# Attention stage: a third place for groups of key pages, and one ring of four PSUM banks for what PE turns or scores

## The chip, the core and the metric

The kernel runs on one core of a Trainium2 chip. The metric is the device time of one execution in microseconds (us). Five engines work side by side, each in its own written order: PE (TensorE, matrix products and transposes), DVE (VectorE), ACT (ScalarE), POOL (GpSimd) and SP (SyncE, which here only issues DMAs). They meet through semaphores. PE writes only to PSUM, which has eight banks of 512 fp32 columns on 128 partitions; DVE and ACT copy results out of it.

## What is computed

One step of a decoder layer with two branches, sparse attention and a recurrent one (RWKV), for a prompt of 1024 rows and for 8 batches of 8 new rows each, which also look back on 2048 cached keys. The change touches only the attention of both. Its part of the reference, cut to what matters:

```python
def _sparse_attention(q, k_sel, v_sel, dist, rel_bias):
    ...
    logits = jnp.einsum('bthd,btkhd->bthk', q, k_sel).astype(jnp.float32) * ATT_SCALE
    logits = logits + jnp.moveaxis(bias, -1, -2)
    logits = jnp.where(valid[:, :, None, :], logits, -jnp.inf)
    probs = jax.nn.softmax(logits, axis=-1)
    return jnp.einsum('bthk,btkhd->bthd', probs.astype(v_sel.dtype), v_sel)
```

The kernel does not gather the selected keys: an earlier stage makes a mask, and the attention runs over all keys with the mask added. For the new rows, keys and values lie in pages of 128 rows of a cache in HBM, and a page table says which 16 pages belong to a batch.

## The kernel before, in words

The program is a row of stages with barriers between them. The attention stage (`attention`, L1735 on) lies between the recurrent branch and the merge with the MLP. It weaves two bodies of work on every engine.

**The prompt.** For each of four pairs of heads `i`: q, k and v come by DMA, PE turns v and k into rows (L1945, three groups each, kept by ACT at L2101 as `v_rows`, `k_rows`). Then come 8 tiles `t` of 128 queries: logits (PE L1906), mask and bias and row maximum (DVE L2192 to L2208), exp (ACT L2108), the turn of the probabilities (PE L1914, one group of up to four 128x128 transposes per head and 512 keys), their copy to `probs_T` (ACT L2101), and the product with v (PE L1926) and with the inverse row sum (PE L1932).

**The sample.** For each of 8 batches `b` there are four groups `j` of four key pages, numbered `J = 4b + j`. SP loads a group into `k_pages` (four DMAs of 256 KB, L1835), which has two places, so that group `J` may be loaded when PE has turned group `J-2` (`k_turned`). PE turns a group in four steps `c` (`turn_keys`, L1977), into the two banks `k_group_T_ps`; DVE copies the even steps (L2253), ACT the odd ones (L2142). `scores` (L1990) multiplies by the queries into the one bank `group_logits_ps`, and DVE masks it (L2267, L2268). `scores_new` (L1996) does the 64 new keys in the same bank. After the exp of the batch (ACT L2152), five groups of probabilities are turned in the same bank again (L2008, L2011), copied by DVE (L2301, L2303) and ACT (L2159), and multiplied by the value pages (L2026). The 16 value pages of a batch are loaded at L1848, a quarter when the same quarter of the batch in front has been used (`v_used`). The mask of a batch is loaded at L1858 when the last batch's masks are done (`masked_new`).

**Banks.** `turn_ps` has one bank for all turns of the prompt: a turn waits until ACT has copied the turn in front (`free_turn`). `k_group_T_ps` has two, `group_logits_ps` one, `logits_ps` two, `att_ps` and `sample_att_ps` one each: eight in all.

**The order.** Every engine's body is a set of generators, each yielding a place on one axis before each piece, and `weave` merges them by that number. One unit is one batch of the sample; a pair of heads takes 2.11 units. On PE key step `c` of group `j` stands at `b + 0.2 j + 0.05 c`, its scores at b plus 0.30, 0.52, 0.72 or 0.92, `scores_new` at `b + 0.93`, the probabilities from `b + 1.10`, the values from `b + 1.34`. On SP the key group stands at `b + 0.2 j - 0.18`, the values at `b + 0.37` (0.65 for the first batch), the mask at `b - 0.03`, the pair's v at `2.11 i - 0.35` and its k and q at `2.11 i - 0.01`. SP issues strictly in that order, so that a wait there holds back all behind it.

## Time and profile before

| | us |
|---|---|
| median of 3 runs | 2878.05 |
| lowest and highest | 2874.58, 2878.06 |
| the profiled execution | 2863.94 |
| its span on the core | 2862.2 |
| attention, from PE's first turn to its last | 1357.5 to 1790 |

The page gives each engine's busy time over the span; the stages differ, so the views that matter are those cut to the attention stage: busy time by stretch, what each engine waited for, and the instructions in order of time. In these, a row of PE is a group of equal matrix instructions with its start, its length, and in brackets how long PE was idle before it and what released it. The granted clock is given as a share of TensorE's full 2.4 GHz; it has two levels, 0.50 (1.2 GHz) and 1.00. The profiled execution lies 14 us under the median of the timed runs.

### The profile page before, as it was taken

What the parts mean: (1) busy time and instruction counts of PE and PEld (TensorE: products, weight loads), DVE (VectorE), ACT (ScalarE), POOL (GpSimd) and SP (SyncE); (2) the same over time, 40 slices, a digit from 0 to 9 for tenths busy, and PEclk for the clock granted to TensorE, in tenths of its full rate; (3) what the DMA queues carried; (4) which work ended last, traced back from release to release, by engine and by line L of the source; (5) the groups of instructions that cost most, each with busy time, mean ns of one, the idle gap of its engine ahead of it and who ended that gap; (6) DMA issues with size and microseconds to landing.
All of it is one profiled execution on the core that took longest, in us unless ns stands there. A gap on an engine that the chain in (4) does not pass through costs nothing. (4 is left out here: it accounts for less than half of the span.)

```text
span 2862.2 us, 52506 instructions
## 1 busy us (share of the span) xinstructions
PE 2516.2 (88%) x21869; PEld 1821.2 (64%) x21869; DVE 1467.6 (51%) x2995; ACT 554.9 (19%) x1170; POOL 92.7 (3%) x133
## 2 busy tenths in 40 slices
PE   6989999777877878876867877999999999999998
PEld 4566666445555456554544545778888888888886
DVE  3449999851642722714634544575543443443543
ACT  3211000022212312321433433212200100100101
POOL 0110000000100100100100100000000000000000
PEclk9989999888898987988988999999999999999999
DMA  5414222231321311212754663631111111111111
GB/s 166 116 27 154 76 76 76 82 116 33 91 75 57 84 58 55 80 32 76 249 190 144 215 208 108 215 107 45 45 30 45 44 45 40 34 45 45 45 30 70
DMA packets 289078, 252.39 MB, mean 88 GB/s; under 512 B 53527, under 2 KB 240505, under 8 KB 288718
## 3 DMA queue, kind: packets, MB, share of 16 engines
q1 hardware_dynamic: 208502, 187.67, 21.8%
q10 hardware_dynamic: 80344, 61.41, 7.2%
q8 instruction: 173, 2.83, 0.4%
q14 instruction: 59, 0.48, 0.1%
HBM read 200.43 MB, written 48.59 MB: 87 GB/s over the span
## 5 line engine op out<-in xcount | busy, mean ns | idle before, releaser
L502 PE MATMUL first_banks<-hT,w_pr 128*128 128x384 f32 (+3 forms) x1392 | 442.1, 479 | 5.3 <-PEq L178 5.3
L502 PEld LDWEIGHTS first_banks<-hT,w_pr 128*128 128x128 f32 (+1 forms) x1392 | 265.0, 192 | 176.7 <-issue 24.5
L989 PE MATMUL rwkv_banks<-h_chunk,w_gate 128*128 128x384 f32 (+1 forms) x768 | 298.3, 534 | 29.1 <-ACT gate_rows L1326 13.3
L2436 DVE TENSOR_TENSOR x<-x,ps_mm 128x272 f32<-128x272 f32 x280 | 120.9, 436 | 308.1 <-PE ps_mm L2403 308.0
L989 PEld LDWEIGHTS rwkv_banks<-h_chunk,w_gate 128*128 128x128 f32 x768 | 155.8, 214 | 124.6 <-issue 57.2
L2403 PE MATMUL ps_mm<-merged_then_hidden,w_mm 128*128 128x272 f32 x960 | 227.1, 393 | 1.6 <-DVE sums_of_right_sides L2656 0.9
L2403 PEld LDWEIGHTS ps_mm<-merged_then_hidden,w_mm 128*128 128x128 f32 x960 | 182.2, 190 | 39.9 <-DVE sums_of_right_sides L2656 1.3
L2403 PE MATMUL ps_mm<-v_T_and_gates_then_h_mlp,w_mm 128*128 128x272 f32 x864 | 204.5, 392 | 0.0
L2427 ACT COPY merged_then_hidden<-ps_mm 128x272 f32<-128x272 f32 x160 | 61.7, 386 | 721.2 <-PE ps_mm L2403 721.2
L2403 PEld LDWEIGHTS ps_mm<-v_T_and_gates_then_h_mlp,w_mm 128*128 128x128 f32 x864 | 164.1, 190 | 33.9
L751 DVE TENSOR_SCALAR_CACHE_REDUCE idx_pages<-scores,mid 128x384 f32<-128x384 f32 (+1 forms) x180 | 170.2, 946 | 6.4
L2403 PE MATMUL ps_mm<-sums_of_right_sides,w_sums_mm 128*128 128x272 f32 x704 | 165.3, 392 | 0.2 <-DVE sums_of_right_sides L2614 0.2
L2403 PEld LDWEIGHTS ps_mm<-sums_of_right_sides,w_sums_mm 128*128 128x128 f32 x704 | 133.7, 190 | 28.1 <-issue 0.6
L2436 DVE TENSOR_TENSOR merged_then_hidden<-merged_then_hidden,ps_mm 128x272 f32<-128x272 f32 x120 | 51.5, 434 | 195.2 <-PE ps_mm L2403 195.2
L1977 PE MATMUL k_group_T_ps<-ident,k_pages 128*128 128x128 f32 x512 | 91.7, 309 | 44.4 <-DMA k_pages<-in_cache_k 44.4
L2403 PE MATMUL ps_mm<-att_T,w_sums_mm 128*128 128x272 f32 x544 | 128.1, 392 | 0.0
L2403 PEld LDWEIGHTS ps_mm<-att_T,w_sums_mm 128*128 128x128 f32 x544 | 103.4, 190 | 21.3
L1977 PEld LDWEIGHTS k_group_T_ps<-ident,k_pages 128*128 128x128 f32 x512 | 65.0, 157 | 72.3 <-DMA k_pages<-in_cache_k 47.5
L2253 DVE COPY k_group_T<-k_group_T_ps 128x512 f32<-128x512 f32 x64 | 44.1, 689 | 106.4 <-PE k_group_T_ps L1977 106.0
L617 ACT COPY stage_pr<-first_banks 128x384 f32<-128x384 f32 (+1 forms) x72 | 33.4, 464 | 325.6 <-PE first_banks L502 325.6
L2403 PE MATMUL ps_mm<-sums_of_right_sides,w_mm 128*128 128x272 f32 x352 | 84.8, 393 | 1.6 <-DVE merged_then_hidden L2436 1.6
L2403 PEld LDWEIGHTS ps_mm<-sums_of_right_sides,w_mm 128*128 128x128 f32 x352 | 66.7, 190 | 16.1 <-DVE merged_then_hidden L2436 2.5
(443 smaller groups left out, 3684.3 us busy)
## 6 DMA issues: line engine op xcount, KB each, us to landing
k_pages<-in_cache_k SPq DMA_DIRECT2D x128, 256.0 KB, 3.1
v_pages<-in_cache_v SPq DMA_DIRECT2D x128, 256.0 KB, 4.6
w_gate<-in_w_in ACTq DMA_DIRECT2D x48, 512.0 KB, 4.0
w_mm<-in_w_mlp_in SPq DMA_DIRECT2D x32, 512.0 KB, 5.4
w_mm<-in_w_mlp_out SPq DMA_DIRECT2D x32, 512.0 KB, 5.3
w_pr<-in_w_in SPq DMA_DIRECT2D x27, 512.0 KB, 6.0
proj_T<-stage_pr ACTq DMA_DIRECT2D x24, 548.0 KB, 5.6
v_T_and_gates_then_h_mlp<-gates_T SPq DMA_DIRECT2D x16, 544.0 KB, 4.7
```

What stands on the lines that cost most here:

```text
L502: ins = MM(B[0:width, 6 + q % 2, 0:m], wk[:, k, 0:width], p.hT[:, k, t0:t0 + m], start=(k == 0), stop=(k == KO - 1))
L617: nc.scalar.copy(dst[:, t0:t0 + m], B[0:width, 6 + q % 2, 0:m]).then_inc(S["kept"], 1)
L751: ch.mark(nc.vector.tensor_scalar(above[0:m, 0:x.shape[1]], x, mid[0:m, j:j + 1], 0.0, ALU.is_gt, ALU.add, accum_out=cnt[0:m, j:j + 1]))
L989: ins = MM(B[:, GB, 0:w], gw[:, n % 2, k, :], hc[:, k, 0:w], start=(k == 0), stop=(k == KO - 1))
L1977: ins = nc.tensor.transpose(KT[:, c % 2, g * 128:g * 128 + 128], kp[:, J % 2, g, c * 128:c * 128 + 128], p.ident[:, :])
L2253: V.tensor_copy(ktb[:, J % 2, c, :], KT[:, 0, :]).then_inc(S["kt_dve"], 1)
L2403: ins = self.nc.tensor.matmul(self.ps[:, c, self.BANK[step], 0:272], left[step][:, k, :], right[step][:, k, 272 * c:272 * c + 272], start= ...
L2427: self.nc.scalar.copy(self.target(step, rows, c), self.out(act, u, step, c)).then_inc(self.by_act, 1)
L2436: self.nc.vector.tensor_tensor(to, to, ps, ALU.add).then_inc(self.by_dve, 1)
```

## The change

`k_pages` gets three places. SP puts every key group 0.2 units earlier (`-0.38` for `-0.18`), and waits for the turn of group `J-3` where it waited for that of `J-2`. The banks `turn_ps` (1), `k_group_T_ps` (2) and `group_logits_ps` (1) become one tensor `turned_or_scored_ps` of four banks. Everything that PE turns or scores takes the next bank in PE's order (`take`), and waits until the bank's last user, four takes before, has been copied or masked. The consumers on ACT and DVE read the bank that `take` has noted. The number of banks stays at eight. There are 329 takes: 120 turns of the prompt, 128 of keys, 32 scores, 8 scores of new keys, 40 turns of probabilities and one of the new values.

```diff
@@ -1749,7 +1749,7 @@
     NQ, QP = 4, NPG // 4
     W = QP * PAGE
     ids = sb("page_ids_kv", [1, NB * NPG], I32)
-    kp, vp = sb("k_pages", [128, 2, QP, HA * DH]), sb("v_pages", [128, NPG, HA * DH])
+    kp, vp = sb("k_pages", [128, 3, QP, HA * DH]), sb("v_pages", [128, NPG, HA * DH])
...
     L = p.ps("logits_ps", [128, 2, 512], own)
-    T = p.ps("turn_ps", [128, 512], own)
     O = p.ps("att_ps", [128, 512], own)
-    KT = p.ps("k_group_T_ps", [128, 2, 512], own)
-    X = p.ps("group_logits_ps", [128, 512], own)
+    R = p.ps("turned_or_scored_ps", [128, 4, 512], own)
     M = p.ps("sample_att_ps", [128, 512], own)
     OS, BK = M[:, 0:128], M[:, 128:256]
...
-    k_in = [p.sem(f"at_k_in{j}") for j in range(2)]
+    k_in = [p.sem(f"at_k_in{j}") for j in range(3)]
     v_in = [p.sem(f"at_v_in{j}") for j in range(NQ)]
     HS = [slice(64 * h, 64 * h + 64) for h in range(2)]
+    bank = {}
...
             def keys():
                 for J in range(NB * NQ):
                     b, j = divmod(J, NQ)
-                    yield b + 0.2 * j - 0.18
-                    if J >= 2:
-                        sp.wait_ge(S["k_turned"], (J - 1) * HP)
+                    yield b + 0.2 * j - 0.38
+                    if J >= 3:
+                        sp.wait_ge(S["k_turned"], (J - 2) * HP)
                     for g in range(QP):
                         n = b * NPG + j * QP + g
                         pages[n] = sp.value_load(ids[0:1, n:n + 1], min_val=0, max_val=cache_k.shape[0] - 1)
-                        sp.dma_start(kp[:, J % 2, g, :],
+                        sp.dma_start(kp[:, J % 3, g, :],
                                      cache_k[ds(pages[n], 1), :, :, :].rearrange("a p h d -> (a p) (h d)"))\
-                            .then_inc(k_in[J % 2], 16)
+                            .then_inc(k_in[J % 3], 16)
...
-            def free_turn(i, key):
-                n = i * NTURN + number[key]
-                if n:
-                    pe.wait_ge(S["turn_kept"], n)
+            left = []
+
+            def take(key, kept, count):
+
+                if len(left) >= 4:
+                    pe.wait_ge(*left[len(left) - 4])
+                bank[key] = len(left) % 4
+                left.append((kept, count))
+                return R[:, bank[key], :]
+
+            def take_turn(i, key):
+                return take((i, key), S["turn_kept"], i * NTURN + number[key] + 1)
 
             def logits(G, n):
                 i, t = divmod(G, NI)
@@ -1909,9 +1916,9 @@
             def turn_probs(G, h, g):
                 i, t = divmod(G, NI)
                 pe.wait_ge(S["exped"], 2 * G + h + 1)
-                free_turn(i, ("p", t, h, g))
+                to = take_turn(i, ("p", t, h, g))
                 for j in range(4 * g, min(4 * g + 4, t + 1)):
-                    ins = nc.tensor.transpose(T[:, (j % 4) * 128:(j % 4) * 128 + 128],
+                    ins = nc.tensor.transpose(to[:, (j % 4) * 128:(j % 4) * 128 + 128],
                                               lg[:, (2 * G + h) % 4, j * 128:j * 128 + 128], p.ident[:, :])
                 ins.then_inc(S["turned"], 1)
...
@@ -1969,12 +1976,10 @@
             def turn_keys(b, j, c):
                 J = b * NQ + j
                 if c == 0:
-                    pe.wait_ge(k_in[J % 2], (J // 2 + 1) * 16 * QP)
-                n = J * HP + c
-                if n >= 2:
-                    pe.wait_ge(S["kt_act" if c % 2 else "kt_dve"], n // 2)
+                    pe.wait_ge(k_in[J % 3], (J // 3 + 1) * 16 * QP)
+                to = take(("keys", J, c), S["kt_act" if c % 2 else "kt_dve"], 2 * J + c // 2 + 1)
                 for g in range(QP):
-                    ins = nc.tensor.transpose(KT[:, c % 2, g * 128:g * 128 + 128], kp[:, J % 2, g, c * 128:c * 128 + 128],
+                    ins = nc.tensor.transpose(to[:, g * 128:g * 128 + 128], kp[:, J % 3, g, c * 128:c * 128 + 128],
                                               p.ident[:, :])
                 ins.then_inc(S["k_turned"], 1)
 
@@ -1982,33 +1987,27 @@
                 J = b * NQ + j
                 pe.wait_ge(S["kt_act"], (J + 1) * 2)
                 pe.wait_ge(S["kt_dve"], (J + 1) * 2)
-                if j:
-                    pe.wait_ge(S["masked"], J)
-                elif b:
-                    pe.wait_ge(S["p_dve"], 3 * b)
+                to = take(("scores", b, j), S["masked"], J + 1)
                 for c in range(HP):
-                    ins = MM(X[32 * c:32 * c + 32, :], qb[:, b, c, :], ktb[:, J % 2, c, :], start=True, stop=True)
+                    ins = MM(to[32 * c:32 * c + 32, :], qb[:, b, c, :], ktb[:, J % 2, c, :], start=True, stop=True)
                 ins.then_inc(S["scored"], 1)
 
             def scores_new(b):
-                pe.wait_ge(S["masked"], b * NQ + NQ)
+                to = take(("new", b), S["masked_new"], b + 1)
                 for c in range(HP):
-                    ins = MM(X[32 * c:32 * c + 32, 0:TS], qb[:, b, c, :], ka[:, c, :], start=True, stop=True)
+                    ins = MM(to[32 * c:32 * c + 32, 0:TS], qb[:, b, c, :], ka[:, c, :], start=True, stop=True)
                 ins.then_inc(S["scored_new"], 1)
...
             def turn_sample_probs(b, q_):
-                if q_ == 0:
-                    pe.wait_ge(S["s_exped"], b + 1)
-                elif q_ % 2:
-                    pe.wait_ge(S["p_dve"], 3 * b + q_ // 2 + 1)
-                else:
-                    pe.wait_ge(S["p_act"], 2 * b + q_ // 2)
+                pe.wait_ge(S["s_exped"], b + 1)
+                to = take(("probs", b, q_), *((S["p_act"], 2 * b + q_ // 2 + 1) if q_ % 2 else
+                                              (S["p_dve"], 3 * b + q_ // 2 + 1)))
                 if q_ < NQ:
                     for g in range(QP):
-                        ins = nc.tensor.transpose(X[:, g * 128:g * 128 + 128],
+                        ins = nc.tensor.transpose(to[:, g * 128:g * 128 + 128],
                                                   ls[:, b % 2, (q_ * QP + g) * 128:(q_ * QP + g) * 128 + 128], p.ident[:, :])
                 else:
-                    ins = nc.tensor.transpose(X[0:TS, 0:128], ls[:, b % 2, PAST:NKS], p.ident[:, :])
+                    ins = nc.tensor.transpose(to[0:TS, 0:128], ls[:, b % 2, PAST:NKS], p.ident[:, :])
                 ins.then_inc(S["p_turned"], 1)
...
-                    dst, src = pt[:, m % 8, 0:w], T[:, 0:w]
+                    dst, src = pt[:, m % 8, 0:w], R[:, bank[i, key], 0:w]
                 nc.scalar.copy(dst, src).then_inc(S["turn_kept"], 1)
...
-                        nc.scalar.copy(ktb[:, J % 2, c, :], KT[:, 1, :]).then_inc(S["kt_act"], 1)
+                        nc.scalar.copy(ktb[:, J % 2, c, :], R[:, bank["keys", J, c], :]).then_inc(S["kt_act"], 1)
```

On PE, DVE, ACT and POOL the order of instructions is the same as before, apart from the bank that each names; only the waits differ. PE at the end of the second batch (b = 1), before; the names are those of the section on the kernel:

```order
L1914 MATMUL turn_ps<-ident,logits 128x128 x4
L1977 MATMUL k_group_T_ps<-ident,k_pages 128x128 x4
L1914 MATMUL turn_ps<-ident,logits 128x128 x12
L1990 MATMUL group_logits_ps<-k_group_T,q_block_diag 32x512 x4
L1996 MATMUL group_logits_ps<-k_new_T,q_block_diag 32x64 x4
L1926 MATMUL att_ps<-probs_T,v_rows 64x128 x8
```

PE at the same place in the changed kernel (its lines are some 7 further down):

```order
L1921 MATMUL turned_or_scored_ps<-ident,logits 128x128 x4
L1982 MATMUL turned_or_scored_ps<-ident,k_pages 128x128 x4
L1921 MATMUL turned_or_scored_ps<-ident,logits 128x128 x12
L1992 MATMUL turned_or_scored_ps<-k_group_T,q_block_diag 32x512 x4
L1998 MATMUL turned_or_scored_ps<-k_new_T,q_block_diag 32x64 x4
L1933 MATMUL att_ps<-probs_T,v_rows 64x128 x8
```

Nothing moved there; the seven groups (four turns of probabilities, one of keys, two scores) now go round four banks instead of keeping to their own.

SP between the value pages of b = 1 and the mask of b = 2, before; four loads of `k_pages` are one group (each with its own register loads, of which the first is shown):

```order
L1848 DMA v_pages<-in_cache_v 128x512 x12
L1846 TENSOR_LOAD page_ids_kv
...
L1848 DMA v_pages<-in_cache_v 128x512
L1834 TENSOR_LOAD page_ids_kv
...
L1835 DMA k_pages<-in_cache_k 128x512
L1811 DMA att_v<-proj_T 128x1088
L1834 TENSOR_LOAD page_ids_kv
...
L1835 DMA k_pages<-in_cache_k 128x512
L1858 DMA mask_of_batch<-mask_of_sample 16x2112 x4
```

SP at the same place in the changed kernel:

```order
L1834 DMA k_pages<-in_cache_k 128x512
L1847 DMA v_pages<-in_cache_v 128x512 x16
L1833 TENSOR_LOAD page_ids_kv
...
L1834 DMA k_pages<-in_cache_k 128x512
L1810 DMA att_v<-proj_T 128x1088
L1833 TENSOR_LOAD page_ids_kv
...
L1834 DMA k_pages<-in_cache_k 128x512
L1857 DMA mask_of_batch<-mask_of_sample 16x2112 x4
```

Before, the group behind the values is group 3 of the same batch, and the one in front of the mask is group 0 of the next. Now all four groups of the batch stand in front of its values, and groups 0 and 1 of the next batch stand between them and the mask. The four register loads for the last value pages are gone, since the pages' numbers are known by then.

At the stage's start SP's row before is `in` loads, v of the first pair, key group 0, mask, k, q, group 1. Now it is:

```order
L1861 DMA k_new_T<-proj_T 128x4x64
L1833 TENSOR_LOAD page_ids_kv
...
L1834 DMA k_pages<-in_cache_k 128x512
L1810 DMA att_v<-proj_T 128x1088
L1833 TENSOR_LOAD page_ids_kv
...
L1834 DMA k_pages<-in_cache_k 128x512
L1857 DMA mask_of_batch<-mask_of_sample 16x2112 x4
L1814 DMA att_k<-proj_T 128x1088
L1815 DMA att_q<-proj_T 128x1088
```

Group 0 moved in front of v, and group 1 in front of the mask, k and q.

## Rows read from the trace of the kernel before

**Rows 1.** The page, part 1: busy time, share of the span, instructions of each engine.

```profile
PE 2516.2 (88%) x21869; PEld 1821.2 (64%) x21869; DVE 1467.6 (51%) x2995; ACT 554.9 (19%) x1170; POOL 92.7 (3%) x133
```

**Rows 2.** Attention: length; busy PE, PEld, DVE, ACT, POOL; clock; DMA share; GB/s.

```profile
1357.50:1790.00 432.50, 328.21 (x3324) 214.46 (x3324) 206.18 (x785) 171.24 (x350) 40.63 (x64) 0.90 0.58 186
```

**Rows 3.** PE's waits, 1357 to 1794: who waited for whom: total, times, longest.

```profile
PE k_group_T_ps L1977 <- DMA k_pages<-in_cache_k: 44.4, 10, 9.3
PE turn_ps L1914 <- ACT probs_T L2101: 19.8, 31, 1.9
PE group_logits_ps L1996 <- DVE group_max L2268: 10.2, 8, 1.5
PE sample_att_ps L2032 <- DVE att_of_heads L2312: 6.0, 8, 2.1
...
PE turn_ps L1945 <- ACT k_rows L2101: 2.8, 5, 0.8
...
PE group_logits_ps L2008 <- DVE probs_by_key L2301: 2.3, 5, 0.6
...
PE turn_ps L1945 <- ACT v_rows L2101: 1.4, 2, 0.7
```

**Rows 4.** PE in order of time: first and last of its seven long key waits.

```profile
1435.95 1.11 PE L1977 MATMUL k_group_T_ps<-ident,k_pages 128*128 128x128 f32 x4 [5.70 <-DMA k_pages<-in_cache_k]
...
1756.32 1.11 PE L1977 MATMUL k_group_T_ps<-ident,k_pages 128*128 128x128 f32 x4 [4.96 <-DMA k_pages<-in_cache_k]
```

**Rows 5.** SP's queue in order of time, before the first of these waits.

```profile
1417.51 11.05 SPq L1848 DMA_DIRECT2D v_pages<-in_cache_v  x16
1429.34 3.65 SPq L1835 DMA_DIRECT2D k_pages<-in_cache_k  x4
```

**Rows 6.** All engines by stretch, columns as in Rows 2.

```profile
1417.50:1436.00 18.50, 12.08 (x172) 7.98 (x172) 7.65 (x30) 3.79 (x7) 1.10 (x2) 0.96 0.93 307
```

**Rows 7.** PE, ACT and DVE in order of time, end of batch 1.

```profile
1444.92 0.63 PE L1914 MATMUL turn_ps<-ident,logits 128*128 128x128 f32 x4 [0.77 <-ACT probs_T L2101]
...
1446.87 1.06 PE L1990 MATMUL group_logits_ps<-k_group_T,q_block_diag 128*32 128x512 f32 x8
1449.09 0.32 PE L1996 MATMUL group_logits_ps<-k_new_T,q_block_diag 128*32 128x64 f32 x8 [1.16 <-DVE group_max L2268]
...
1445.58 0.59 ACT L2101 COPY probs_T<-turn_ps 128x512 f32<-128x512 f32 x1 [0.81 <-PE turn_ps L1914]
...
1448.34 0.69 DVE L2268 CUSTOM_DVE_ANT_0 logits_of_batch<-group_logits_ps,mask_of_batch 128x512 f32<-128x512 f32 x1
```

**Rows 8.** PE in seven stretches at the low clock: length, busy, clock, DMA share.

```profile
1434.50:1441.30 6.80, 5.35 (x32) 0.50 0.78 259
...
1755.30:1762.20 6.90, 5.88 (x26) 0.51 0.03 10
sum 47.80, PE 33.27; mean PE 4.75
```

**Rows 9.** PE in the other five such stretches: the longest, and the sum.

```profile
1560.70:1574.40 13.70, 10.87 (x62) 0.50 0.28 76
...
sum 34.30, PE 29.82; mean PE 5.96
```

**Rows 10.** PE in order of time: eight key transposes at the low and at the full clock.

```profile
1438.90 1.97 PE L1977 MATMUL k_group_T_ps<-ident,k_pages 128*128 128x128 f32 x8
...
1452.19 1.09 PE L1977 MATMUL k_group_T_ps<-ident,k_pages 128*128 128x128 f32 x8
```

**Rows 11.** The stage's start in order of time: SP's queue, then PE.

```profile
1353.59 3.70 SPq L1835 DMA_DIRECT2D k_pages<-in_cache_k  x4
...
1359.20 0.42 SPq L1815 DMA_DIRECT2D att_k<-proj_T  x1
...
1362.98 1.12 PE L1977 MATMUL k_group_T_ps<-ident,k_pages 128*128 128x128 f32 x4 [2.38 <-DMA k_pages<-in_cache_k]
...
1366.73 0.63 PE L1945 MATMUL turn_ps<-ident,att_k 128*128 128x128 f32 x4 [0.68 <-ACT v_rows L2101]
```

More of the change, by code:

```diff
@@ L1941, in prompt @@
                                 pe.wait_ge(S["in_" + name], i * 16 + 16)
-                            free_turn(i, (name, g))
+                            to = take_turn(i, (name, g))
                             for j in range(4 * g, min(4 * g + 4, NI + 1)):
                                 w = 128 if j < NI else TS
-                                ins = nc.tensor.transpose(T[0:w, (j % 4) * 128:(j % 4) * 128 + 128],
+                                ins = nc.tensor.transpose(to[0:w, (j % 4) * 128:(j % 4) * 128 + 128],
                                                           rows[:, j * 128:j * 128 + w], p.ident[:, :])
@@ L2036, in sample @@
                 pe.wait_ge(S["in"], 48)
+                to = take("values", S["vn_made"], 1)
                 for c in range(HP):
-                    ins = nc.tensor.transpose(X[0:TS, c * 128:c * 128 + 128], va[:, c, :], p.ident[:, :])
+                    ins = nc.tensor.transpose(to[0:TS, c * 128:c * 128 + 128], va[:, c, :], p.ident[:, :])
                 ins.then_inc(S["vn_turned"], 1)
@@ L2090, in keep_turned @@
                         act.wait_ge(S["out_made"], NI * i)
-                    dst, src = rows[0:w, 4 * key[1]:4 * key[1] + a, :], T[0:w, 0:a * 128]
+                    dst, src = rows[0:w, 4 * key[1]:4 * key[1] + a, :], R[0:w, bank[i, key], 0:a * 128]
                     src = src.rearrange("p (a c) -> p a c", a=a)
@@ L2147, in probs @@
                 act.wait_ge(S["v_zero"], 1)
-                nc.scalar.copy(vn[0:TS, :], X[0:TS, :]).then_inc(S["vn_made"], 1)
+                nc.scalar.copy(vn[0:TS, :], R[0:TS, bank["values"], :]).then_inc(S["vn_made"], 1)
                 for b in range(NB):
@@ L2158, in probs @@
                             act.wait_ge(S["out"], b)
-                        nc.scalar.copy(pr[:, q_ * QP:q_ * QP + QP, :].rearrange("p g c -> p (g c)"), X[:, :])\
-                            .then_inc(S["p_act"], 1)
+                        nc.scalar.copy(pr[:, q_ * QP:q_ * QP + QP, :].rearrange("p g c -> p (g c)"),
+                                       R[:, bank["probs", b, q_], :]).then_inc(S["p_act"], 1)
             weave(prompt(), keep_keys(), probs())
@@ L2252, in keep_keys @@
                             dve.wait_ge(S["scored"], J - 1)
-                        V.tensor_copy(ktb[:, J % 2, c, :], KT[:, 0, :]).then_inc(S["kt_dve"], 1)
+                        V.tensor_copy(ktb[:, J % 2, c, :], R[:, bank["keys", J, c], :]).then_inc(S["kt_dve"], 1)
             def mask(b, j):
@@ L2258, in mask @@
                 dve.wait_ge(S["scored"], J + 1)
+                X = R[:, bank["scores", b, j], :]
                 if j == 0:
@@ L2267, in mask @@
                     ch.done(V.tensor_tensor(tail, tail, p.near_k[:, 0:128], ALU.add))
-                V.tensor_tensor_reduce(out=ls[:, s, j * W:j * W + W], in0=X[:, :], in1=mk[:, j * W:j * W + W],
+                V.tensor_tensor_reduce(out=ls[:, s, j * W:j * W + W], in0=X, in1=mk[:, j * W:j * W + W],
                                        scale=1.0, scalar=NEG, op0=ALU.add, op1=ALU.max, accum_out=mxs[:, s, j:j + 1])\
@@ L2274, in mask_new @@
                 dve.wait_ge(S["scored_new"], b + 1)
+                X = R[:, bank["new", b], :]
                 own_ = X[:, b * ST:b * ST + ST]
@@ L2299, in attend @@
                             dve.wait_ge(S["out"], b)
+                        X = R[:, bank["probs", b, q_], :]
                         if q_ < NQ:
-                            ins = V.tensor_copy(pr[:, q_ * QP:q_ * QP + QP, :].rearrange("p g c -> p (g c)"), X[:, :])
+                            ins = V.tensor_copy(pr[:, q_ * QP:q_ * QP + QP, :].rearrange("p g c -> p (g c)"), X)
                         else:
```

## The prediction

> **What bounds the kernel now.** The page comes first: PE is busy for 88% of the span and no other engine for more than 51% [rows 1], so time is won where PE stands still or runs slowly. The only stage that the change touches is the attention, and the view of busy time by stretch cuts it out: 432.5 us, of which PE is busy 328.2 us, at a mean clock of 0.90; DVE is busy 206 us and ACT 171 us [rows 2]. PE is thus idle for 104 us there, the other two for over half of it, so neither is the bound by amount of work.
>
> The view of waits says what the 104 us are made of [rows 3]. The largest is 44.4 us in 10 waits for key pages. Then come waits for a bank: 19.8 us (31 times) and 2.8 and 1.4 us in which a turn of the prompt waits for ACT's copy of the turn in front; 10.2 us (8 times, once per batch) in which the scores of the new keys wait for DVE's mask on the last page group; and 2.3 us for turns of probabilities. These bank waits sum to 36.5 us. What is left is real dependence, such as the 6.0 us before the turn of the finished rows, and the change does not touch it.
>
> In order of time the key waits are not spread out. Seven of them, 5.70 us at 1435.95 to 4.96 us at 1756.32, one for each batch but the first, all stand before the same instruction, the first turn of group 3 [rows 4]. SP's queue shows why: the 16 value pages are issued from 1417.51 and group 3 only behind them, from 1429.34; its last page lands 6.6 us later [rows 4, 5]. In that stretch the DMA engines are 0.93 busy and move 307 GB/s [rows 6]. So group 3 is late because 4.2 MB of values stand in front of it, not because its place comes free late.
>
> The clock view adds a cost that no list of waits holds. Around each of these seven stalls TensorE is granted 0.50, which is 1.2 GHz: 47.8 us in all, with 33.3 us of PE work in them [rows 8]. Five more such stretches hold 29.8 us of work [rows 9]. Eight key transposes take 1.97 us at the low level and 1.09 us at the full one [rows 10]: the same work is 45% shorter.
>
> **The change part by part.**
>
> *Keys.* The third place alone lets SP load a group further ahead; the earlier number in the order puts it there. At every slot but one SP now loads one group more than before while waiting for the same turned group, because J went up by one and the distance from 2 to 3. The exception is what counts: group 3 now stands in front of the values and group 0 of the next batch behind them. Group 3 then has the time from 0.22 to 0.60 units, which at 45 us per unit is 17 us, against 3.65 us of issue [rows 5] and a few us to land. Group 0 behind the values stands at 0.62 and is needed at 1.00, again 17 us. The values take 11.05 us of issue from about 0.38 and the group 3.65 us, which ends at 0.71 units; where the prompt's rows are stored in between, some 4 us later, which with a few us to land still leaves about 5 us. Nothing is late next that I can see: the values themselves are used one unit later. So of the 44.4 us the 2.38 us of the stage's start [rows 11] are counted below and 42.0 us can go. Bounds: 34 us if group 0 inherits about 1 us per batch (the seven waits of group 3 average 5.8 us, and the transfers are as dense as in [rows 6]), 42 us if all goes. I take 40, near the upper end, since the slack is several times the load.
>
> *Ring.* A turn of the prompt starts 0.77 us late because the bank is being copied, 0.59 us on ACT [rows 7]. With four banks it starts at once, and ACT's copy moves up too. The gain holds only as far as PE has other work in front of the instruction that needs the copies. In the run of four turns and a key turn before 1446.87, ACT must still make five copies of 0.59 us and its own small gaps, so PE can run ahead by at most four and then goes at ACT's pace, some 0.65 us a turn instead of 0.63 + 0.77 = 1.40: most of the wait goes there. In the first, short tiles the product needs the copy at once, and there the wait only moves behind the second turn. The scores of the new keys no longer wait for the mask (end 1449.03 after scores that began at 1446.87) and have long free work behind them: that wait goes nearly whole, 9 of 10.2. Of the other 26.3 us I take 15. Sum 24. Bounds: 9 us (only the mask wait) and 36.5 us (all). A new wait: a take now waits for whatever used the bank four takes ago. Behind it on PE is everything; who waits for that is ACT and DVE, which idle anyway. Two takes last 1.09 us on PE, four thus 2.2 us [rows 10], and a copy is done about 0.8 us after its turn, a mask about 2.2 us after its scores began [rows 7]. So only scores can be met again too early, 40 times, by some 0.4 us where DVE is behind and no product lies between; one nearly always does. I cost it at nothing; without the products as cover it would be 40 x 0.4 = 16 us, which takes the term from 24 to 8, just under its lower bound.
>
> *Clock.* If the seven stalls go, the low stretches around them should go: 33.3 x 0.45 = 15.0 us. If all twelve go, 63.1 x 0.45 = 28.4 us. If the clock finds other small gaps to fall in, 0. I take 12, near the seven, since the longest of the other five, 13.7 us [rows 9], has no key stall at all, and such will stay.
>
> Beside this the Trainium skill has a warning that speaks against the ring: "TensorE: Matmul & The Clock Gate", section "A second HAM failure mode: psum-queue depth-cycling", tells of a kernel whose cycling through PSUM banks makes TensorE idle for very short times between groups, so that its clock swings. What it would make of this sum is the last rival. The rows at hand show short waits of 0.77 us inside a stretch at the full clock [rows 7], and low stretches around long ones, so this trace leans against it, with [rows 9] the part that it could claim.
>
> *Start.* Group 0 now precedes v, and group 1 precedes mask, k and q. Group 0 is issued 3.7 us a group [rows 11], so PE's wait of 2.38 us for it may vanish, but v comes about as much later; and k and q, used without a wait at 1366.73 after an issue at 1359.20, come 3.7 us later. Between a gain of 2.4 and a loss of 5 us; I take a loss of 1, as the DMA engines are full here and only the order changes.
>
> *The rest.* Four register loads per batch on SP are gone, hidden. PE, DVE, ACT and POOL keep their instructions and order.
>
> Sum: 40 + 24 + 12 - 1 = 75 us. The profiled execution's 2863.9 us becomes 2789. It lies 14 us below the median of the timed runs, and those are what the result is compared with: 2878 - 75 = 2803 us.
>
> **The rivals.**
>
> *The waits change hands (chance 0.19).* PE's stalls of 5.8 us let ACT and DVE catch up; without them PE meets their latency at once, and the ring and the clock bring nothing. For it: ACT's and DVE's work is 171 and 206 us in a stage of about 357 us, and both work in strict order. Against it: their largest waits are for PE, not for each other. Only the keys' 40 us are won: 2838 us.
>
> *Keys stay late (0.08).* With the stage shorter the same bytes need 186 x 432 / 357 = 225 GB/s on average, and group 0 of the next batch behind the values waits as group 3 did. Then the keys and their clock bring nothing and the ring its 24 us: 2854 us. Against: 17 us of time per group, and 307 GB/s shown as possible [rows 6].
>
> *More than all (0.03).* Every bank wait and all low stretches go: 42 + 36.5 + 28.4 + 2.4 = 109 us, 2769 us.
>
> *The ring holds back (0.04): slower.* Before, a key turn waited only for its own copy two steps back, and never for DVE's mask or for a slow prompt copy. Now one late consumer in DVE's row blocks every kind of turn. With the mean bank wait of today, 19.8 / 31 = 0.64 us, the gain of 75 us is used up when 117 of the 329 takes are met too early, 37 more than the 80 of scores and probabilities. If 150 were, the time would be 2878 - 75 + 96 = 2899 us. Against: the hold times above.
>
> *The clock swings (0.02): slower.* Short idle times at bank changes keep the clock down. PE's work outside the twelve low stretches is 328.2 - 63.1 = 265 us. If 150 us of it ran at the low level, it would cost 150 x (1.97 / 1.09 - 1) = 121 us against 63 won without the clock term: 2936 us. In the Trainium skill this is the case of the section named above.
>
> *No change, the rest (0.02).* The third place is not used since something else on SP, such as the wait for `masked_new`, sets when keys are issued, and the ring is filled up by ACT's pace.
>
> **How the numbers follow.** My forecast has 0.62. Its own bounds: 34 + 15 + 0 - 5 = 44 us at the poor end (2834), 42 + 34 + 25 = 101 us at the good one (2777). The range reaches to the first rival and leaves out the others, which hold 0.19 together: 2777 to 2840. A measurement of this kernel can tell about 0.2%, 6 us. Faster by more: 0.62 + 0.19 + 0.08 + 0.03 = 0.92. Within: 0.02. Slower: 0.04 + 0.02 = 0.06.
>
> **What would show it.** In the profile after, the attention stretch should last about 358 us. PE's wait for key pages should fall from 44.4 to under 5 us, and none should stand behind the values; if one of over 3 us stands before group 0 of a batch, the second rival is at work. The wait of prompt turns for `probs_T` should fall from 19.8 to about 10 us; if the products' own wait for `probs_T` has grown by as much, the first rival is. The wait of `scores_new` for the mask should be gone. The low-clock stretches at the seven stalls should be gone and the mean clock be about 0.95. PE's total of waits for DVE's masks (releases of `masked`) tells whether the ring holds back. Wrong I would be most likely in the size of the ring's and the clock's terms, since both rest on how much work lies between a turn and its use.

## The result

The changed kernel takes 2777.87 us (median of 4 runs, 2763.86 to 2781.08) against 2878.06 us for the kernel before: a ratio of 0.9643 (95% interval 0.9608 to 0.9679). It was forecast faster and is, but by 100 us where 75 were forecast; the ratio times the 2878.05 us that the forecast started from is 2775 us, 2 us beyond the good end of the range (2777). The ratio is formed over all runs; the two medians alone would give 0.9652, thus 2778 us, so the miss of the range is smaller than the noise, but the miss of the 75 us is not. The mechanisms named were right; the term for the clock was far too small, and a cost that goes with it was not in the sum.

In the profiles the span falls from 2862.2 to 2778.4 us. All of it lies in the attention stage. From PE's first turn (L2038) to its last (L2031 after, L2032 before) the stage lasts 1361.64 to 1703.95, thus 342.3 us after 432.3, which is 90.0 us less. The other 6 us of difference to the span are 4 us more ahead of the stage and 2 us more behind it, where no instruction changed. So 90 us are shown by the pair of profiles, and the 100 us of the medians hold some 10 that it does not show. The profiled execution of the kernel before took 2863.94 us, 14 us less than the median of its timed runs here and 7 to 9 less than its medians in the later experiments (2871 to 2872 us), while that of the changed kernel lies 2 us over its own; that is about the size of the 10. They are less than the spread of the changed kernel's own runs (17 us).

The row of the stage after the change, which answers to [rows 2] (columns as there):

```profile
1361.60:1704.00 342.40, 297.20 (x3324) 202.56 (x3324) 203.50 (x785) 168.11 (x350) 40.66 (x64) 0.96 0.72 235
```

PE's busy time went from 328.2 to 297.2 us with the same 3324 instructions, and its idle time from 104.3 to 45.2. The mean clock went from 0.90 to 0.96 and the rate of the DMAs from 186 to 235 GB/s. What PE still waits for there (the view of waits, who for whom, total, times, longest) answers to [rows 3]:

```profile
PE turned_or_scored_ps L1952 <- DMA att_k<-proj_T: 11.2, 3, 6.0
PE sample_att_ps L2031 <- DVE att_of_heads L2315: 6.7, 8, 2.1
PE att_ps L1933 <- ACT probs_T L2101: 6.0, 8, 1.1
PE att_ps L1939 <- DVE inverse_on_diagonal L2214: 4.0, 7, 0.9
...
PE turned_or_scored_ps L2007 <- ACT probs_T L2101: 2.8, 2, 1.5
PE turned_or_scored_ps L1952 <- DMA att_v<-proj_T: 2.8, 1, 2.8
...
PE turned_or_scored_ps L1982 <- DVE group_max L2269: 1.1, 2, 0.6
...
PE turned_or_scored_ps L1921 <- ACT probs_T L2101: 0.2, 1, 0.2
```

The key pages, 44.4 us before, are not in the list at all. The wait of the prompt's turns for `probs_T`, 19.8 us before, is 0.2 us (the last row). Waits for a bank are down to about 5 us in all: the row of 1.1 us, in which a key turn meets a bank that DVE's mask still holds, the 2.8 us in which a turn of the sample's probabilities meets one that ACT is copying to `probs_T`, and four of 0.4 us or less. New is the wait for k and v of the prompt, 14.0 us where k alone had 3.7.

SP's queue in order of time, the place of [rows 5], shows the values issued with nothing urgent behind them; the group after them is that of the next batch:

```profile
1420.03 8.82 SPq L1847 DMA_DIRECT2D v_pages<-in_cache_v  x16
1429.62 3.97 SPq L1834 DMA_DIRECT2D k_pages<-in_cache_k  x4
```

PE in order of time goes from the last step of group 2 of batch 1 (first row) to the first step of group 3 (second row) without a wait for its pages, where it had 5.70 us [rows 4]:

```profile
1431.09 0.66 PE L1982 MATMUL turned_or_scored_ps<-ident,k_pages 128*128 128x128 f32 x4
...
1432.70 0.66 PE L1982 MATMUL turned_or_scored_ps<-ident,k_pages 128*128 128x128 f32 x4
```

PE at the end of batch 1, the place of [rows 7], which shows the second of three waits for the bank. The other two were, before:

```profile
1443.53 0.63 PE L1914 MATMUL turn_ps<-ident,logits 128*128 128x128 f32 x4 [0.41 <-ACT probs_T L2101]
...
1446.31 0.63 PE L1914 MATMUL turn_ps<-ident,logits 128*128 128x128 f32 x4 [0.77 <-ACT probs_T L2101]
```

And now:

```profile
1436.79 0.66 PE L1921 MATMUL turned_or_scored_ps<-ident,logits 128*128 128x128 f32 x4 [0.38 <-ACT logits L2108]
1437.28 0.60 PE L1982 MATMUL turned_or_scored_ps<-ident,k_pages 128*128 128x128 f32 x4
1437.71 1.47 PE L1921 MATMUL turned_or_scored_ps<-ident,logits 128*128 128x128 f32 x12
1439.12 1.07 PE L1992 MATMUL turned_or_scored_ps<-k_group_T,q_block_diag 128*32 128x512 f32 x8
1440.00 0.29 PE L1998 MATMUL turned_or_scored_ps<-k_new_T,q_block_diag 128*32 128x64 f32 x8
```

Three groups of four turns run as one row of 12 in 1.47 us, where they had 0.41, 0.77 and 0.77 us of idle in front; the scores of the new keys follow the last group's at once. From the scores' start (L1992) to that of the new keys (L1998) it is 0.88 us, where it was 1449.09 - 1446.87 = 2.22 us.

The three stretches of the stage at the low clock (PE only: length, busy, clock, DMA share, GB/s):

```profile
1361.60:1377.10 15.50, 9.26 (x42) 0.50 0.89 294
1452.20:1459.00 6.80, 5.73 (x30) 0.50 0.51 191
1554.60:1558.00 3.40, 3.40 (x14) 0.50 1.05 394
sum 25.70, PE 18.39; mean PE 6.13
```

Of the twelve behind the start [rows 8, 9], with 63.1 us of PE work in them, two are left with 9.1 us. The stretch at the start has become longer. It holds the waits of 2.8 and 3.4 us for v and k, and the one at 1452.20 stands around the longest wait that is left, for k of the second pair:

```profile
1453.27 1.11 PE L1952 MATMUL turned_or_scored_ps<-ident,att_k 128*128 128x128 f32 x4 [5.97 <-DMA att_k<-proj_T]
```

### The profile page after: what moved, and what is told of

The parts are those of the page before. It is cut to its first block and busy times, and to the rows that moved or that the text cites. A ratio compares the mean times of both kernels' runs of the same rounds, so it can differ in the third digit from the quotient of the medians.

```text
span 2778.4 us, 52435 instructions
## 1 busy us (share of the span) xinstructions
PE 2487.6 (90%) x21869; PEld 1812.8 (65%) x21869; DVE 1465.6 (53%) x2995; ACT 551.4 (20%) x1170; POOL 93.0 (3%) x133
## 3 DMA queue, kind: packets, MB, share of 16 engines
q1 hardware_dynamic: 208502, 187.67, 22.4%
## 5 line engine op out<-in xcount | busy, mean ns | idle before, releaser
L989 PE MATMUL rwkv_banks<-h_chunk,w_gate 128*128 128x384 f32 (+1 forms) x768 | 296.9, 532 | 29.2 <-ACT gate_rows L1326 13.3
L1982 PE MATMUL turned_or_scored_ps<-ident,k_pages 128*128 128x128 f32 x512 | 83.2, 288 | 2.0 <-DVE group_max L2269 1.1
L2406 PE MATMUL ps_mm<-merged_then_hidden,w_sums_mm 128*128 128x272 f32 x320 | 76.6, 392 | 0.0
L1982 PEld LDWEIGHTS turned_or_scored_ps<-ident,k_pages 128*128 128x128 f32 x512 | 58.8, 145 | 26.1 <-issue 18.9
```

Source lines behind the costliest of these rows:

```text
L989: ins = MM(B[:, GB, 0:w], gw[:, n % 2, k, :], hc[:, k, 0:w], start=(k == 0), stop=(k == KO - 1))
L1982: ins = nc.tensor.transpose(to[:, g * 128:g * 128 + 128], kp[:, J % 3, g, c * 128:c * 128 + 128], p.ident[:, :])
L2406: ins = self.nc.tensor.matmul(self.ps[:, c, self.BANK[step], 0:272], left[step][:, k, :], right[step][:, k, 272 * c:272 * c + 272], start= ...
```

## The experiments

Times are medians. The kernel before, run beside them, had medians of 2871 to 2872 us, so the ratios are the better comparison. "Stage" is from PE's first turn to its last in the profile. It comes from one execution each, and two executions of the changed kernel differ by 4 us in it (last row).

| kernel | us | ratio to before | stage, us | PE busy in it |
|---|---|---|---|---|
| before | 2878.1 | 1 | 432.3 | 328.2 |
| changed | 2777.9 | 0.9643 (0.9608 to 0.9679) | 342.3 | 297.2 |
| keys_only | 2817.3 | 0.9808 (0.976 to 0.9856) | 383.2 | 314.9 |
| ring_only | 2846.4 | 0.9913 (0.9886 to 0.994) | 404.8 | 312.7 |
| two_places | 2806.2 | 0.9761 (0.9708 to 0.9814) | 369.0 | 303.3 |
| old_slot | 2842.4 | 0.9907 (0.9878 to 0.9937) | 404.6 | 315.8 |
| ring_of_3 | 2788.4 | 0.9704 (0.9669 to 0.9739) | 353.4 | 305.5 |
| ring_of_2 | 2834.6 | 0.9863 (0.9828 to 0.9898) | 393.3 | 323.3 |
| start_order | 2769.5 | 0.963 (0.9594 to 0.9667) | 339.2 | 298.7 |
| kq_early | 2755.1 | 0.9582 (0.9546 to 0.9618) | 330.4 | 298.9 |
| two_places_kq | 2776.9 | 0.9678 (0.9655 to 0.9701) | 340.5 | 300.8 |
| filled_stalls | 2861.5 | 0.9963 (0.9947 to 0.998) | 432.5 | 348.4 |
| changed_again | 2767.8 | 0.9657 (0.9622 to 0.9691) | 338.2 | 295.8 |

### Each half alone

keys_only is the kernel before with

```diff
-    kp, ... = sb("k_pages", [128, 2, QP, HA * DH]), ...
+    kp, ... = sb("k_pages", [128, 3, QP, HA * DH]), ...
-                    yield b + 0.2 * j - 0.18
-                    if J >= 2:
-                        sp.wait_ge(S["k_turned"], (J - 1) * HP)
+                    yield b + 0.2 * j - 0.38
+                    if J >= 3:
+                        sp.wait_ge(S["k_turned"], (J - 2) * HP)
```

and `J % 3` for `J % 2` wherever `kp` or `k_in` is meant.

> The kernel before with the keys' part of the change alone: three places and the earlier slot, old banks. Theory A (the terms add up): the 44.4 us of key waits go and with them the seven low-clock stretches that stand around them (33.3 us of PE work, 15 us); the bank waits of 36.5 us stay. Attention 432 -> about 375 us, the whole 55 to 60 us faster than before (ratio about 0.980). Theory B (the ring is what lets PE use the keys): only 30 us or less, since PE then waits for banks instead. Four to six low-clock stretches should be left under A.

Theory A held in the main: 55 us faster by the ratio (interval 41 to 69). The stage is 49.1 us shorter, 383 us where some 375 were expected; of the missing 8, some 6.6 are longer waits for the prompt's k and v (10.3 us after 3.7). No wait for key pages is left, the waits for banks are as before (21.2 us for `probs_T`, 10.2 for the mask), and all seven low-clock stretches around the old stalls are gone. Five are left behind the start; four of them stand at nearly the same instructions as four of the other five of before [rows 9], the fifth behind the waits for v and k at the start.

ring_only is the changed kernel with that same edit undone.

> The changed kernel with the keys' part undone: ring of four banks, two places and the old slot. Theory A (terms add): bank waits go, about 25 us of idle time, key waits stay at 44 us: 25 to 30 us faster than before. Theory B (the gain is eaten): group 3 lands when the values in front of it have landed, whatever PE does, so PE only arrives earlier at the same stall; key waits grow from 44 to 55 or 60 us and the gain is 10 to 15 us.

25 us faster, but the trace shows why it is not more, and there theory B was right: the key waits have grown.

```profile
PE turned_or_scored_ps L1982 <- DMA k_pages<-in_cache_k: 57.0, 13, 7.8
PE turned_or_scored_ps L1952 <- DMA att_k<-proj_T: 7.0, 1, 7.0
```

They rose from 44.4 to 57.0 us [rows 3]: 12.6 us of what the banks gave went into arriving earlier at the same transfers. PE's idle time fell by only 12.0 us; its busy time fell by 15.5. The two halves alone shorten the stage by 49.1 and 27.5 us, together by 90.0. The 13.4 us above their sum have the size of this eaten part, which comes free once the keys are no longer late; no run isolates it.

### Place or order

two_places is the changed kernel with two places for key groups but the early slot, old_slot the one with three places and the old slot (`- 0.18`).

> The changed kernel with only two places for key groups, but the earlier slot, so that SP waits for the turn of group J-2 a little longer and group 3 still stands in front of the values. Theory A (the order on SP is what counts, as group 3 was late behind the values): within 10 us of the changed kernel (2778 to 2790 us), key waits under 5 us. Theory B (the place counts): SP blocks on the turn, all behind it is late, and at least half of the 44 us of key waits comes back: 2800 us or more.

> The changed kernel with three places and the ring but the old slot, -0.18. Theory A (order counts): group 3 again stands behind the values, the seven key waits come back with 35 to 45 us and with them low-clock stretches; about 2830 us, near ring_only. Theory B (the place counts): the third place hides it, within 10 us of the changed kernel.

old_slot settles the larger question: with the third place and the old order, 55.5 us of key waits are there (35 to 45 were expected; ring_only has 57.0), and its stage is that of ring_only, 404.6 against 404.8 us. The place by itself is worth nothing. two_places missed both limits that I had set for theory A: it is 28 us slower than the changed kernel, which is the time that theory B gave, but the key waits are 14.8 us and not half of the 44. Its waits, in order of size (the wait for `k_new_T`, which stands before the stage in all kernels, left out):

```profile
PE turned_or_scored_ps L1952 <- DMA att_k<-proj_T: 23.6, 4, 8.3
...
PE turned_or_scored_ps L1982 <- DMA k_pages<-in_cache_k: 14.8, 5, 6.9
```

With two places SP stands at the early slot until group J-2 is turned. The view of what SP's queue waited for shows it, first in the changed kernel, then in two_places:

```profile
SPq L1833 <- PE turned_or_scored_ps L1982: 6.7, 6, 4.0
SPq L1833 <- PE turned_or_scored_ps L1982: 89.0, 20, 13.5
```

What stands behind it is late: mostly the prompt's k (12.4 us more than in the changed kernel), and key groups. So the order removes the stall behind the values, with or without a third place, and the third place is what keeps SP from blocking there.

### How many banks

ring_of_3 and ring_of_2 are the changed kernel with 3 or 2 for 4 in `take`; the banks left over are unused.

> The changed kernel with a ring of three banks (one bank unused). Theory A (hold time decides): a copied bank is free about 0.8 us after its turn and three takes last 1.6 us on PE, so only scores, held 2.2 us by DVE's mask, are met too early: 3 to 10 us slower than the changed kernel, waits on consumers in PE's list up by that much, mostly on group_max. Theory B (every bank counts alike): a third or more of the ring's gain of some 45 us is lost: 15 us or more slower.

> The changed kernel with a ring of two banks (two unused). Theory A (hold time): two takes last 1.1 us, just over a copy's 0.8 us but under a mask's 2.2 us; about 40 takes meet a mask for 1 us each and many a copy for 0.3 us: 50 to 80 us slower than the changed kernel, near keys_only with its dedicated banks (2817 us) or worse. Theory B (most of the ring's gain is that turns of different kinds alternate): under 25 us slower.

With two banks theory A held. With three the result lies between the two theories: 10.5 us slower by the medians and 11 us of stage, just over the 3 to 10 of theory A, but 14 to 18 us by the ratios to the kernel before (0.9704 against 0.9657 and 0.9643, with intervals that overlap), where theory B began at 15. The waits for a bank sum to about 11 us after 5; their largest rows are

```profile
PE turned_or_scored_ps L1982 <- ACT probs_T L2101: 3.1, 3, 1.7
...
PE turned_or_scored_ps L1921 <- DVE group_max L2269: 2.2, 3, 0.9
```

So it was not mostly the mask, as I had expected, but the copies too. PE's idle time grew by 2.8 us only; its busy time grew by 8.3, and in this execution the low clock of the start lasted to 1385.9, so part of the 11 us may be the execution and not the bank. Two banks lose 51 us of stage, and their stage is longer than with four banks with fixed owners (393.3 against 383.2 us of keys_only, which has the same keys). So sharing alone is no gain where the ring is that short.

### What PE waits for now

kq_early moves the prompt's loads on SP ahead of the keys and the mask; start_order does so for the first pair only.

```diff
-                    yield 2.11 * i - 0.35
+                    yield 2.11 * i - 0.40
-                    yield 2.11 * i - 0.01
+                    yield 2.11 * i - 0.36
```

> The changed kernel with the pair's v at 2.11 i - 0.40 and its k and q at 2.11 i - 0.36 in SP's order, thus v in front of key group 0 at the start, and k and q in front of group 1 and of the mask. Theory A (k, q and v are what PE waits for now, 11.2 and 2.8 us): these 14 us go and the low clock at the stage's start gets shorter by 5 to 10 us (2 to 4 us of work): 10 to 16 us faster than the changed kernel, about 2764 us. Theory B (the transfers are the limit there): what k and q gain, key groups lose, within 4 us of the changed kernel.

> The changed kernel with that same earlier place of v, k and q for the first pair of heads only. Theory A: the start's share goes, 2.8 and 3.4 us of waits for v and k, less up to 3 us for key group 1: 3 to 7 us faster than the changed kernel. Theory B (the start is bound by bytes): within 2 us of it.

kq_early is faster still, 2755.1 us, so theory B is out. Its ratio 0.9582 lies below that of both timings of the changed kernel, though its interval touches that of the first; the difference is 18 to 22 us, more than the 10 to 16 of theory A. The stage is 11.9 us shorter, which lies within them. The gain is PE's idle time, 31.5 us after 45.1; PE is busy for 298.9 us after 297.2, as the low stretch at the start is shorter but others came later in the stage. The one DMA that PE waits for within the stage is

```profile
PE turned_or_scored_ps L1982 <- DMA k_pages<-in_cache_k: 0.8, 1, 0.8
```

start_order gives 3.1 us of stage, at the lower end of theory A; by its ratio it can't be told from the changed kernel. The waits for v and k at the start, 6.2 us, go; 1.0 us for key groups and 1.5 us more busy time of PE come, and the later pairs' k costs 8.1 us in two waits, as before (7.9).

> The kernel with early k, q and v (kq_early) but two places for key groups. Theory A (without the third place the loss is that SP blocks on a turn and k and q stand behind it): with k and q in front, half or more of the 28 us that two_places lost comes back: 2765 to 2780 us. Theory B (the loss is the late key groups themselves): 20 us or more above kq_early's 2755, and key waits of 15 us or more.

The median, 2776.9 us, lies in the range of theory A and, 22 us above kq_early, also over the limit of theory B; the limits that I had set overlap, so the time does not decide. By the stage, two places cost 10.1 us with k and q in front instead of 26.7, so some 17 us of the loss would be late k; what is left has the size of the 11.4 us of key waits. By the ratios the cost went only from 34 to 28 us. The split is thus open, and both parts exist.

### Does the stall lower the clock

filled_stalls puts work into the stalls of the kernel before:

```diff
+                if j == 3 and c == 0 and b:
+                    pe.wait_ge(S["done"], 2 * b)
+                    for _ in range(30):
+                        nc.tensor.transpose(M[:, 256:384], p.ident[:, :], p.ident[:, :])
                 if c == 0:
                     pe.wait_ge(k_in[J % 2], (J // 2 + 1) * 16 * QP)
```

> The kernel before with 30 extra transposes of the identity (about 4.1 us of PE work at the full clock, into unused columns, read by nobody) in front of the first turn of key group 3 of each batch but the first, where PE waits for the pages anyway. Theory A (the stall is what lowers the clock, and the low clock costs extra PE time behind it): the seven low stretches at these places go, the waits fall to 1 or 2 us each, and although PE does 29 us more work the whole is 8 to 18 us faster than before. Theory B (the low stretches come from the short bank waits and transposes, not from these stalls): they stay, and the time is the same as before or up to 5 us more.

The added row before the first stall, and the wait that is left of it:

```profile
1436.36 3.49 PE L1974 MATMUL sample_att_ps<-ident 128*128 128x128 f32 x30
1443.20 0.66 PE L1981 MATMUL k_group_T_ps<-ident,k_pages 128*128 128x128 f32 x4 [3.35 <-DMA k_pages<-in_cache_k]
```

The 30 transposes took 3.49 us, not 4.1, so stalls of up to 4.4 us remained. The low stretches around these stalls got shorter, but most did not go:

```profile
1444.60:1448.00 3.40, 3.40 (x22) 0.50 0.59 214
...
sum 27.30, PE 25.81; mean PE 3.69
```

These are 27.3 us with 25.8 us of work. One of the seven windows summed there, at 1489.00, lies ahead of the added row of its batch (1495.25) and does not belong to a stall; the fourth stall has no low stretch any more. That leaves six with 22.4 us of work, after 33.3 [rows 8], and two of these six begin only 5 and 9 us behind the end of their stall. With 10.9 us less work at the low level, 5 us are expected. By the runs it is 0.37% faster (0.2 to 0.5%), 10 us, though PE does 7 x 3.49 = 24 us more work; by the stage in the profile it is the same as before. There the low stretch at the stage's start, which the edit does not touch, holds 17.7 us of work after 5.2, which at 45% hides 5.6 us. So a filled stall lowers the clock less, which speaks for theory A, but its size is not settled by this run. The stronger evidence that the stalls lower the clock is keys_only: the bank waits stayed, the stalls went, and all seven stretches went with them.

> The changed kernel as it is, on the chip of these runs. The attention stage again 342 us within 1, PE busy 297 us in it, ratio to the kernel before 0.964 within its interval; the ratio by the stage alone would be (432 - 342) / 2872 = 0.969, so a value of 0.969 or more says that the first comparison was some 10 us lucky, and one near 0.964 that there is a gain that the two profiles do not show.

The stage came out at 338.2, not within 1 us of 342.3, and the ratio at 0.9657. Two executions of the same program thus differ by 4 us in this stage; the low stretches explain part of it, since at the start of the stage one execution has the low clock for 15.5 us and the other for 12.2. Both of the expected values for the stage and PE's work (342 and 297 us, measured 338.2 and 295.8) were set too narrow. The timing agrees with the first one.

## Why the prediction fell 25 us short, step by step

Of the 25 us, 15 are in the profiles (90 us of stage for 75) and are explained here; the other 10 are those that the pair of profiles does not show.

**Keys: 40 forecast, all 44.4 went** (42.0 and the start's 2.4). Reading SP's queue, not the number of places, was right: group 3 was late behind the values. The inheritance by group 0 did not come, with DMAs at 235 GB/s on average; old_slot and two_places show that it is the order that counts.

**Ring, idle time: 24 forecast, 25 measured.** PE's idle time fell by 59.1 us; 44.4 are the keys, and the waits for the prompt's k and v rose from 3.7 to 14.0, so 59.1 - 44.4 + 10.3 = 25.0 are left for the ring. The sum is right, its parts less so: the prompt's turns wait 0.2 us for `probs_T`, where about 10 were expected to stay, and more than expected came back as dependence: products waiting for `probs_T` went from 3.9 to 6.0 us, for the inverse from 1.6 to 4.0, and the turns of the sample's probabilities for their exp from 1.6 to 3.2. That the two errors cancel is luck. What the forecast did not see is that alone the ring keeps only half of the 25 us, as the waits for the key pages grow. That it holds back, the slower rival, did not happen with four banks, nor as a loss against the kernel before with two.

**Clock: 12 forecast, 31.0 measured as less busy time of PE. This is the step that failed**, "I take 12, near the seven, since the longest of the other five, 13.7 us [rows 9], has no key stall at all, and such will stay". All seven went, and of the other five three went too, the longest among them; ten of twelve in all. It was right only for the keys' part alone, since keys_only still has the longest one, at nearly the same instructions and without a key stall:

```profile
1544.90:1555.20 10.30, 8.38 (x51) 0.50 0.27 74
```

In ring_only 3.4 us of work are left of it, in the changed kernel nothing. So these three were not fixed; they went when both parts together had taken the idle times around them. Why the clock falls just there is not shown. Work at the low clock, the start included, fell from 68.0 to 18.4 us; at 45% [rows 10] that is 22 us. The other 9 us are a cost that I had not listed, a term put at nothing: a group of four transposes by itself is busy for 0.66 us, but joined to others each adds less (1.09 us for two, 1.47 for three). Each removed bank wait joins two groups, and some 50 waits at about 0.17 us (0.63 + 0.63 - 1.09) make 8.7 us. The traces show it directly, as PE's order is the same in both and its 3324 instructions can be set side by side: those that ran at the full clock both times are busy 8.7 us less in sum, of which 8.5 us are in the 56 that had an idle time behind them before and have none now; those that changed their clock make 21.6 us. The experiments give the same split: keys_only has 28.6 us less low-clock work, which makes 12.8 of its 13.3 us of busy time gained; ring_only has 17.8 us less, 8.0 of its 15.5, and the remaining 7.5 are joined groups. No run isolates the two. The end of each matrix instruction is modelled in the profile, so where busy time stops and idle time begins at a short wait is as good as that model; the sum of both, the stage, is measured.

**Start: a loss of 1 forecast, 8 measured**, which is 10.3 us more waits for k and v, less the 2.4 for key group 0 counted with the keys. v came 2.8 us and k 3.4 us late at the start, and for the later pairs k cost 7.9 us after 3.7. That part was not in the sum, and with it the loss lies outside the bounds (a gain of 2.4 to a loss of 5): k and q of a later pair stand behind the mask and a key group as before, but PE now gets there sooner. kq_early takes these waits away.

Sum by the profiles: 44.4 + 25.0 - 10.3 + 31.0 = 90.1. Forecast were 40 + 24 - 1 + 12 = 75.

**The range.** Its ends do not use the bounds of the terms: the ring went in with 15 and 34 us, though its bounds were given as 9 and 36.5, and the clock with 25, though 28.4 were possible. With the bounds as given, the ends are 34 + 9 + 0 - 5 = 38 and 42 + 36.5 + 28.4 + 2.4 = 109 us, thus 2840 and 2769, and the good one is the rival "more than all". The measured 2775 lies between. The clock's own 22 us lie within its bounds; the 9 us of joined groups stand in no bound.

The clock rival with its page did not come either. The Trainium skill's "TensorE: Matmul & The Clock Gate", section "A second HAM failure mode: psum-queue depth-cycling", tells of a kernel that goes round its banks and in which PE is idle for very short times between groups so often that the clock swings. Here the ring took such idle times away, and in ring_only the work at the low clock fell from 68.0 to 50.2 us.

## What to carry to other kernels

Where a small transfer is late, look at what stands in front of it in the queue before giving it more room: here the order was worth the whole stall, and the extra place only kept the queue from blocking. Banks shared in a ring gained here with four and lost with two; count the hold time of a bank against the length of n takes. And when PE's stalls go, count the clock and the joined groups as well: here they were a third of the gain. Removing waits of one kind alone can be eaten in part by a transfer that PE only meets sooner.

## What the runs showed of the hardware

The cost of a short wait on PE is more than its idle time. Three groups of four transposes took 1.47 us in a row and 0.63 us each when split by waits; by the two traces, 56 such breaks cost 8.5 us of busy time. The low clock at the stage's start lasted on in spite of work: the stretch to 1377.10 holds 9.26 us of PE work in 15.5 us and stays at 0.50, with two waits for DMAs of about 3 us inside it, while in the dense parts the clock did not fall in over 90 us on end (1459.0 to 1554.6). How long the low clock lasts at the start differs from one execution to the next: the kernel before and filled_stalls have the same instructions there, and that stretch held 5.2 us of work in the one and 17.7 in the other, so differences of a few us between the stages of two profiles are not to be trusted.
